# Attention value products with the values as the loaded side

## The reference

```python
h = rmsnorm(x); proj = h @ w_in        # q, k, v of mixer A; q, latent of B; indexer; gates
# A: 8 heads, 2 shared k/v; each chunk of 64 rows sees its own and the chunk before
p = softmax(concat(q @ k.T / 8 + bias, sink))[..., :-1];  o_a = p @ v
# B: an indexer picks the top 256 keys of each row; 8 heads on one shared k/v
p = softmax(where(selected, q @ k_b.T / 8 + bias, NEG));  o_b = p @ v_b
x = x + (sigmoid(ga) * (o_a @ w_a) + sigmoid(gb) * (o_b @ w_b)) @ w_out
x = x + (silu(h2 @ w_g) * (h2 @ w_u)) @ w_d;  return rmsnorm(x)
```

## Time and profile before

| | |
|---|---|
| median of 3 runs | 3635.88 us |
| profiled execution, its span | 3635.51 us, 3633.6 us |
| PE busy | 3476.2 us (96%) |
| PEld busy | 2879.6 us (79%) |
| DVE busy | 2002.1 us (55%) |
| ACT busy | 1373.1 us (38%) |
| POOL busy | 1622.7 us (45%) |
| mean granted TensorE clock | 0.984 |

### The profile page before, as it was taken

The page is one execution under the profiler, slowest core; times in us unless marked ns, Lnnn a source line. Parts: engine busy times, 40 slices in busy tenths (PEclk is TensorE's granted clock), DMA queues, the critical chain, the costliest instruction groups (busy, mean ns, idle before and its releaser), DMA issues.

```text
span 3633.6 us, 45712 instructions
## 1 busy us (share of the span) xinstructions
PE 3476.2 (96%) x17440; PEld 2879.6 (79%) x17440; DVE 2002.1 (55%) x3579; ACT 1373.1 (38%) x2513; POOL 1622.7 (45%) x916
## 2 busy tenths in 40 slices
PE   8999999999899999899999989999999699999998
PEld 6778778787777887797788768977887589878887
DVE  3236666475754456575565767765677577631112
ACT  3224444353623232462433336624453356420001
POOL 4555454544045666203566640045667200156664
PEclk9999999999999999999999999999999899999999
DMA  5745454455052333304233340052333400133332
GB/s 146 199 127 168 121 166 116 126 175 195 1 170 83 97 93 99 138 1 169 82 93 97 97 161 1 1 197 83 93 96 96 167 1 1 50 121 97 93 99 93
DMA packets 420521, 382.44 MB, mean 105 GB/s; under 512 B 19120, under 2 KB 347056, under 8 KB 419664
## 3 DMA queue, kind: packets, MB, share of 16 engines
q1 hardware_dynamic: 396384, 337.16, 30.5%
q10 hardware_dynamic: 23920, 42.36, 3.3%
HBM read 316.68 MB, written 62.78 MB: 104 GB/s over the span
## 4 chain that ended last, share of the span: by engine, by line
PE 84%; DVE 9%; ACT 3%; issue 2%; DMA 1%; POOL 1%; ACTq 0%; SPq 0%; DVEq 0%; POOLq 0%
PE BANK L589 19%; PE BANK L590 19%; PE BANK L591 19%; PE BANK L794 4%; PE BANK L809 3%; PE BANK L808 3%; PE LP L591 3%; PE LP L589 3%; PE LP L590 3%; PE LP L773 2%; PE LP L774 2%; PE LP L675 2%; PE LP L676 2%; PE LP L779 1%; DVE CSD L1366 1%
## 5 line engine op out<-in xcount | busy, mean ns | idle before, releaser
L563 POOL TENSOR_SCALAR WHI<-WRAW 128x1024 fp32r<-128x1024 f32 x456 | 503.1, 1103 | 1954.9 <-PE BANK L591 1199.8
L565 POOL TENSOR_TENSOR WLO<-WRAW,WHI 128x1024 fp32r<-128x1024 f32 x456 | 1119.8, 2456 | 38.0
L589 PE MATMUL BANK<-H2hi,WHI 128*128 128x512 f32 x1408 | 559.9, 398 | 1.8 <-POOL WLO L565 1.6
L590 PE MATMUL BANK<-H2lo,WHI 128*128 128x512 f32 x1408 | 558.2, 396 | 0.0
L591 PE MATMUL BANK<-H2hi,WLO 128*128 128x512 f32 x1408 | 556.8, 395 | 0.0
L589 PE MATMUL BANK<-HThi,WHI 128*128 128x512 f32 (+1 forms) x1024 | 407.1, 398 | 1.9 <-DVE QS L1274 1.9
L590 PE MATMUL BANK<-HTlo,WHI 128*128 128x512 f32 (+1 forms) x1024 | 405.0, 396 | 0.0
L591 PE MATMUL BANK<-HThi,WLO 128*128 128x512 f32 (+1 forms) x1024 | 404.6, 395 | 0.0
L1032 ACT ACTIVATE MASK<-SCD,THR 128x896 bf16<-128x896 f32 (+5 forms) x186 | 281.9, 1516 | 255.9 <-DVE THR L1333 227.2
L1685 DVE TENSOR_TENSOR BANK<-BANK,SL 128x512 f32<-128x512 f32 x88 | 61.6, 700 | 477.2 <-PE BANK L591 474.2
L589 PEld LDWEIGHTS BANK<-H2hi,WHI 128*128 128x128 f32 x1408 | 265.4, 189 | 67.8 <-issue 2.2
(11 more groups left out here) (241 smaller groups left out, 6807.4 us busy)
## 6 DMA issues: line engine op xcount, KB each, us to landing
WRAW<-in_w_in SPq DMA_DIRECT2D x124, 512.0 KB, 4.3
WRAW<-in_w_ffn_gate SPq DMA_DIRECT2D x88, 512.0 KB, 3.8
WRAW<-in_w_ffn_up SPq DMA_DIRECT2D x88, 512.0 KB, 3.8
WRAW<-in_w_ffn_down SPq DMA_DIRECT2D x88, 512.0 KB, 3.7
qsp<-QS SPq DMA_DIRECT2D x32, 512.0 KB, 5.7
gates<-GS ACTq DMA_DIRECT2D x64, 256.0 KB, 2.2
GL<-gates ACTq DMA_DIRECT2D x64, 256.0 KB, 3.8
WRAW<-in_w_out SPq DMA_DIRECT2D x32, 512.0 KB, 3.9
```

Source lines behind the costliest of these rows:

```text
L563: nc.gpsimd.tensor_scalar(hi, raw, 1.0, 1.0, ALU.mult, ALU.mult).then_inc(w_hi, 1)
L565: nc.gpsimd.tensor_tensor(lo, raw, hi.bitcast(f32), ALU.subtract).then_inc(w_split, 1)
L589: nc.tensor.matmul(dst, whi, mhi, start=first, stop=False)
L590: nc.tensor.matmul(dst, whi, mlo, start=False, stop=False)
```

## The change

The value products swap sides: V is loaded, and the turned probabilities move. A group now holds up to two key tiles of two neighbouring heads (a pair), so that one product moves 256 columns, both heads' 128 query rows. The results stand with V's columns down and query rows across. When four heads are done (two pairs), ScalarE copies the bank to a new tile `XV` (`x_copy`), TensorE turns its four parts back into the same bank (`turn_back`), and VectorE's `outputs` start from there, now waiting for `turned`.

Heads are worked in pairs, so the orders are new: key pieces run two pairs ahead in B (six half units in A), `LG` of B has six buffers instead of four, masks are issued pair by pair, spread over the groups by `paced`, and exponentials alternate between the heads of the next pair, one after each group from the first. `turn_back` stands one group after the last of the four heads, VectorE's `outputs` two groups after, `out_transposes` five.

```diff
-                    for e, (h, kt, _) in enumerate(groups(u)[g]):
-                        dst = values.bank[:, (h % 4) * P:(h % 4 + 1) * P]
-                        v = VA[:, first + kt - b * JT + 1, h // (HEADS // KVH), :] if kind == "a" else VB[:, kt, :]
-                        nc.tensor.matmul(dst, PThi[kind][t % 2][:, e, :], v, start=(kt == 0), stop=False, skip_group_check=True)
...
+                    dst = values.bank[:, p % 2 * 2 * P:(p % 2 + 1) * 2 * P]
+                    r = (n(pt_hi, key) - 1) % 2
+                    pe.wait_ge(pt_ready, n(pt_ready, key))
+                    for e, t in enumerate(groups(b, kind, p)[g]):
+                        v = VA[:, first + t - b * JT + 1, p // 2 % 2, :] if kind == "a" else VB[:, t, :]
+                        nc.tensor.matmul(dst, v, PThi[kind][r][:, 2 * e:2 * e + 2, :].rearrange("p h q -> p (h q)"),
+                                         start=(t == 0), stop=False, skip_group_check=True)
...
+                def turn_back(q):
+
+                    dst = values_bank(("x", b, kind, q))[:, :].rearrange("p (h q) -> p h q", h=4)
+                    pe.wait_ge(x_copied, n(x_copied, (b, kind, q)))
+                    for h in range(4):
+                        last = nc.tensor.transpose(dst[:, h, :], XV[kind][q % 2][:, h, :], IDENT[:, :])
+                    last.then_inc(turned, made(turned, (b, kind, q)))
...
+                seq = all_groups(b, kind)
+                for i, (p, g) in enumerate(seq):
+                    if i + 1 < len(seq):
+                        transposes(*seq[i + 1])
+                    t = p + AHEAD[kind]
+                    for _ in range(paced(b, kind, t, p, g)[0] - (paced(b, kind, t, p, g - 1)[0] if g else 0)):
+                        next(pieces_of_qk)
+                    values(p, g)
+                    for q in range(PAIRS // 2):
+                        if i == after(b, kind, 2 * q + 1, 1):
+                            turn_back(q)
...
+                def x_copy(q):
+                    p = 2 * q + 1
+                    act.wait_ge(values_done, n(values_done, (b, kind, p, len(groups(b, kind, p)) - 1)))
...
+                    if g == 0 and p and p % 2 == 0:
+                        x_copy(p // 2 - 1)
+                    next(ahead, None)
...
+                    nc.vector.tensor_tensor(PTlo[kind][r][:, 0:w, :], trans(key)[:, 0:w, :],
+                                            PThi[kind][r][:, 0:w, :].bitcast(f32), ALU.subtract
+                                            ).then_inc(pt_ready, made(pt_ready, key))
...
+                    t = p + lead
+                    for _ in range(paced(b, kind, t, p, g)[1] - (paced(b, kind, t, p, g - 1)[1] if g else 0)):
+                        next(ahead)
```

More of the change, by code:

```diff
@@ L747, in attend @@
             def attend(b, kind):
-                items = units(b, kind)
-                ends = last_of_rows(b, kind)
                 def qk(u):
@@ L797, in values, with queries_keys @@
[L797 to L804, removed]
-                    for e, (h, kt, _) in enumerate(groups(u)[g]):
-                        dst = values.bank[:, (h % 4) * P:(h % 4 + 1) * P]
-                        v = VA[:, first + kt - b * JT + 1, h // (HEADS // KVH), :] if kind == "a" else VB[:, kt, :]
-                        nc.tensor.matmul(dst, PThi[kind][t % 2][:, e, :], v, start=(kt == 0), stop=False, skip_group_check=True)
-                        last = nc.tensor.matmul(dst, PTlo[kind][t % 2][:, e, :], v, start=False, stop=(kt == tiles - 1),
-                                                skip_group_check=True)
-                    last.then_inc(values_done, made(values_done, (u, g)))
+                def queries_keys():
+                    for u in units(b, kind):
+                        yield from qk(u)
@@ new lines, in transposes @@
+                def transposes(p, g):
+                    grp = groups(b, kind, p)[g]
+                    dst = take("trans", pt_ready, (b, kind, p, g))
+                    for i, u in pair_units(b, kind, p):
+                        s = p % 2 if kind == "a" else grp[0] * P // LGW
+                        pe.wait_ge(probs, n(probs, (u, s)))
+                    for e, t in enumerate(grp):
+                        for h in range(2):
+                            last = nc.tensor.transpose(dst[:, 2 * e + h, :], probabilities(kind, p, h, t), IDENT[:, :])
+                    last.then_inc(trans_full, made(trans_full, (b, kind, p, g)))
@@ new lines, in values @@
+                def values(p, g):
+                    key = (b, kind, p, g)
+                    tiles, first = key_tiles(b, kind, p // 4)
+                    if g == 0 and p % 2 == 0:
+                        values.bank = take("values", o_step, ("o", b, kind, p // 2, 2), ("x", b, kind, p // 2))
+                    dst = values.bank[:, p % 2 * 2 * P:(p % 2 + 1) * 2 * P]
[5 more added lines that the diff above has]
+                                         start=(t == 0), stop=False, skip_group_check=True)
+                        last = nc.tensor.matmul(dst, v, PTlo[kind][r][:, 2 * e:2 * e + 2, :].rearrange("p h q -> p (h q)"),
+                                                start=False, stop=(t == tiles - 1), skip_group_check=True)
+                    last.then_inc(values_done, made(values_done, key))
@@ new lines, in attend @@
+                for p in range(lead):
+                    for _ in exps(p):
+                        pass
+                seq = all_groups(b, kind)
+                for i, (p, g) in enumerate(seq):
+                    key = (b, kind, p, g)
+                    if g == 0:
+                        ahead = exps(p + lead)
+                    r, w = (n(pt_hi, key) - 1) % 2, 2 * len(groups(b, kind, p)[g])
+                    act.wait_ge(trans_full, n(trans_full, key))
+                    if pt_last[r] is not None:
+                        act.wait_ge(values_done, n(values_done, pt_last[r]))
+                    pt_last[r] = key
+                    nc.scalar.copy(PThi[kind][r][:, 0:w, :], trans(key)[:, 0:w, :]).then_inc(pt_hi, made(pt_hi, key))
+                    if g == 0 and p and p % 2 == 0:
+                        x_copy(p // 2 - 1)
+                    next(ahead, None)
+                    if i + 1 == len(seq) or seq[i + 1][0] != p:
+                        for _ in ahead:
+                            pass
+                    for q in range(1, PAIRS // 2, 2):
+                        if i == after(b, kind, 2 * q + 1, 7):
+                            out_copy(q // 2)
```

324 lines of the change are left out of this document (157 added, 167 removed).

## The result

The changed kernel takes 3687.3 us (median of 4 runs, 3685.72 to 3692.91), the kernel before 3635.86 in the same session: ratio 1.0143, 95% interval 1.0125 to 1.016. It is slower, as forecast, but by 51 us and not by 9. The time lies above the range. The profiled execution took 3687.87 us (span 3686.1), at a mean granted clock of 0.98.

The account below looks back on a forecast made before the run. TensorE was taken as the bound, with the new mask order eating its saving. Terms +9.4 - 3.9 + 2.3 - 5 - 7 + 4.5 + 11 + 3 - 6 = +8.3, say +9 on 3635.5: 3645 us, 8-in-10 range 3585 to 3677.

Parts of the forecast that it names:

- The products: Value products, both mixers: half as many, 0.118 us each at 256 columns; -113 us in mixer B, -26 in mixer A.
- The mask chain: Mixer B: logits, mask, lo part, value products set the interval, 2.35 us; block 3 +9.4, block 2 -3.9, block 1 +2.3.
- The ends: Start and end of each mixer: last outputs -7 us, later first transposes +4.5, longer tails +11, lower clock +3.
- First value products of blocks 1 to 3: Mixer B starts: first transposes behind four heads' key products instead of three, needing two more masks, +4.5 us.
- Last outputs: Mixer B blocks 3, 2, 1: last pairs without key products, last output after 20.0, 15.0, 10.0 us; -7.
- the longer tail: End of each mixer: copy, four transposes and two hand-offs before the output transposes, +1.4 us, eight times +11.
- 3.3 was named as a sign: Sign in the new trace: 3.3 us of idle TensorE ahead of the last output transposes of each mixer.
- Block 0: Mixer B, block 0: masks of 512 and less fit under TensorE's 1.75 us, so saved products count; about -5 us.
- Mixer A: Mixer A: VectorE leads, key products gain a head start over their mask; -6 us, bounds -20 and +15.
- rival (2): ScalarE late: XV copy and exponential delay the next cast; +32 us, 3677; 0.15 together with another rival, slower.
- the 3 set aside for the clock: Mixer ends: TensorE runs at the lower clock after idling; +3 us over eight ends (0 to 12).
- Rival (1): Mixer B masks not behind, so the saving shows: -92 us, 3544 in full, 3590 with half the masks binding; chance 0.22.

Follow-up runs that it names:

- Run 8: Changed kernel with masks one group later in mixer B blocks 1 to 3, mixer A's output copy earlier, longer lead in block 0 of mixer B: 3600.38 us, ratio 0.9888.
- run 1: Changed kernel with each mask issued one group later, behind the next group's lo part, in mixer B of blocks 1 to 3: 3626.88 us, ratio 0.9974.
- run 4: Kernel before, its own products, with masks issued one group earlier in block 3 of mixer B alone: 3686.65 us, ratio 1.0133.
- Run 7: Changed kernel; in block 0 of mixer B key products and masks run three pairs ahead, exponentials two, instead of two and one: 3673.65 us, ratio 1.0106.
- run 6: Changed kernel; in mixer A ScalarE issues the copy of the output transposes one group earlier: 3672.99 us, ratio 1.0106.
- run 10: As run 8, with ScalarE's exponentials in mixer B spread over the groups of a pair: 3594.37 us, ratio 0.988.
- run 2: As run 1, with each mask also cut into pieces of up to 512 columns: 3629.82 us, ratio 0.9972.
- run 3: Changed kernel in mixer B, order and products of the kernel before in mixer A: 3666.23 us, ratio 1.007.
- run 9: As run 8, with first transposes of mixer B in blocks 1 to 3 behind three heads' key products instead of four: 3603.93 us, ratio 0.9907.
- run 11: As run 10, with masks of mixer B also cut into pieces of up to 512 columns: 3602.27 us, ratio 0.9898.
- run 5: New products and masks one group later in mixer B blocks 1 to 3; kernel before's code in mixer A and block 0 of mixer B: 3595.03 us, ratio 0.9888.

## Why the prediction was wrong

**The products: right in kind, too cheap in the sum.** Back to back the wide one costs 0.118 where 0.118 was taken. By the rule of the Trainium skill ("TensorE: Matmul & The Clock Gate", section "Wait — 56ns, not 53.3ns?") TensorE's products would have saved nothing. That rule counts the moving columns and no weight load; here every product has a load of its own, the starts lie 0.11 apart at 128 columns and 0.118 at 256, and a group's value products fell from 0.84 to 0.47, so for these products the measurement decides against it. But 0.118 is not what one costs on average. In 87 of block 3's 110 groups of four products the second product starts 0.19 to 0.23 after the first, and the group takes 0.55 to 0.59: in all 55 that stand behind a wait, in all 22 right behind the bias products, and in 10 others. Counted by the distance of starts, without idle time, block 3's value products took 101 us before (0.109 each) and 64 after (0.139 each): 37 saved, where the forecast's prices give 48. In all of mixer B the same count gives about 96 us saved, where 113 was forecast. Run 8, with fewer waits, has 0.135 each.

**The mask chain: right in kind and near in one head's size, too small in the sum.** Predicted at 16 tiles 2.35, 1.75, 2.50, 1.39; measured 2.19, 1.84, 2.41, 1.48. Block 3's six intervals were forecast at 176.6 and took 179.8, block 2's at 122.0 and took 125.9. Block 1 was the largest miss here: 86.8 forecast, 94.2 measured, at 7 and 8 tiles 17.7 to 18.5 per four heads against 16.8 and 17.6. Runs 1 and 4 show the cause by moving the masks alone. What makes block 1's surplus over the chain wasn't taken apart; with masks a group later it is gone (14.0 to 14.7). Together these intervals grew by 22.2 us where +7.8 was forecast.

**The ends: two terms mis-sized, against each other.** First value products of blocks 1 to 3: 7.9 later, where +4.5 was forecast. The first output after them came another 6.4 later, and for that the sum has no term. It isn't the later place of `outputs`, which run 1 shares: from first value product to first output blocks 1 to 3 take 12.8, 20.4 and 28.5 us before, 15.5, 22.0 and 30.6 after, and 12.5, 19.8 and 25.5 in run 1, where only the masks moved. It is the same mask chain in the first four heads, which the forecast counted from the first output on alone. Last outputs: 17.3, 12.4 and 8.5 us, -13.7 where -7 was forecast, and the longer tail, +1.4 each, is already in them, for it lies ahead of the eighth output. From the last value product to the output transposes the eight ends of the two mixers grew by 1.1 to 1.9 us (+1.4 forecast). At the end of mixer A in block 3 it takes 4.1 us, where it took 2.2, and TensorE's idle time in it is 1.87, where 3.3 was named as a sign; the granted clock at the first of these rows is 0.50:

```profile
2957.18 0.41 PE L843 MATMUL BANK<-PTloa,VA 128*128 128x256 f32 x1
...
2961.26 1.09 PE L859 MATMUL BANK<-IDENT,ONa 128*128 128x128 f32 x4 [1.87 <-DVE ONa L1507]
```

**Block 0: the step that failed.** "Masks of 512 and less fit under TensorE's 1.75, so products saved count": -5, where the stretch got 12.6 longer. I asked whether a mask's length fits, and not how far ahead masks and exponentials run where a pair is one or two groups. Run 7 shows it: one more pair of lead for key products, masks and exponentials takes the whole of it back. Which of the three needed it stays open.

**Mixer A: the other.** "VectorE leads there", -6 before the tails. The loss was made in ScalarE's queue: the new copy of the turned bank and the exponentials stand ahead of a copy that frees a bank (run 6, 14 us in the whole time, and mixer A back in the range of the code before). The saving that the -6 stood for didn't show even then. This is rival (2) in another place than the one I priced. Its copy ahead of an exponential was looked for where it delays a cast, and it did its damage where it delays the copy queued last. I named what stands behind VectorE's and TensorE's new waits, and for ScalarE's only the next cast.

In sum: mixer A 14 us more than forecast, block 0 of mixer B 16, blocks 1 to 3 14 (intervals 14, starts 10, less 10 for last outputs and tails), less the 3 set aside for the clock. That the sum was not further off is in part luck: the last outputs and tails missed the other way. Rival (1), the saving, was real, though in mixer B it was about 96 us by the starts and not 113; runs 8 and 10 show 38 to 45 us of it in the whole time. The rest is in turns, starts and tails, and in waits of 15 to 23 us in block 3 that no run took away.

## What to carry to other kernels

When an order is rewritten, write for each hand-off how many groups lie between producer and consumer, before and after, on every engine; a group of slack lost was worth 33 to 50 us in one block here, more than halving the products saved. An instruction added to a queue must be priced by all that stands behind it, the last one too, if that one frees a buffer. A change that gets slower while its bottleneck engine loses work is worth a second look: three moves of order turned +51 us into -38. And before a stage's gain is credited to an edit, compare the same stage in runs that do not touch it: mixer A's unchanged code varied by 8 us between profiles.

## What was not expected of the hardware

The granted clock over block 0 of mixer B was 0.98 before (947 to 1011) and 0.85 after. The waits of that stretch alone don't set it: with the same order of work there it was 0.86 to 0.88 in runs 1 and 2 and 0.91 in runs 3 and 6, which changed only mixer A ahead of it; with run 7's order it was 0.90 to 0.94 (runs 7 to 11), and with the order of the kernel before 0.93 in runs 4 and 5. The lengths fall apart cleanly where the clocks overlap: 74.0 to 76.9 us, 63.5 to 64.6, and 64.3 to 65.3. What makes the clock fall was not isolated. What the lower level costs is seen at its price per product: a 256-column product starts 0.21 after the last (2956.97 to 2957.18, granted clock 0.50) and not 0.12.

Nor was it expected that a group of wide products costs 0.58 instead of 0.47 once it has waited. In the kernel before, the second product of such a group (128 columns) starts 0.14 to 0.15 after the first. No run takes this apart.
